# Two stage entries of a fused fp32-accurate kernel: the last chunk of X turned through VectorE and DMAs, and the first two jobs alternating

## Chip, cores and metric

The kernel runs on one core of one Trainium2 chip. The metric is the device time of one execution in microseconds; the median of three runs is given.

## What is computed

One sequence of 256 tokens, model width 2048, all in float32, goes through a retention layer, a pooling layer, an RMS norm, a block with two kinds of attention, a cross-attention to 256 memory tokens, a gated feed-forward layer and a last RMS norm. What matters for the change are the two places where the running sum x is normalised and enters the next projection:

```python
h = h + retention_layer(h, ...)          # ends in  o @ w_out
h = h + pooling_layer(h, ...)            # begins with rms_norm(h) @ w_in ; ends in @ w_out
x = rms_norm(h, final_norm)
# second block
h = rms_norm_2(x, g_mix); proj = h @ w_in    # dq, dk, dv, c_q, c_kv, k_rope
```

## The kernel before, in words

**Products.** X (256 tokens by 2048) stays in SBUF, in two tiles of 128 tokens. Every float32 product is made of three fp32r products: weights are split into `hi` (ScalarE, `split_hi`, L671) and `lo` = raw - hi (VectorE, `split_lo`, L1173), the activation, turned so that its 2048 features lie on partitions, into `xh` and `xl`. A **job** is 512 output columns for both token tiles (two PSUM banks). A **unit** is 512 rows of weight for one job, 1 MB, in two halves; `unit` (L1983) issues 12 matmuls of 512 columns for each half, 24 for a unit: hi with xh (L1998), hi with xl (L1999), lo with xh (L2004). Jobs alternate between two PSUM pairs (`J % 2`), so a third job can start only when the first is drained.

**Look-ahead.** `hi` and `lo` have four places, one for each half: ScalarE may split half H once TensorE has used half H-4 (`half_used`), which is two units of look-ahead. ScalarE and VectorE run their instructions in program order; whatever waits in their stream holds back the splits that stand behind it. Weights are loaded by SyncE into four raw buffers when `lo` of four units earlier is done.

**Entries.** Two stages end in an output projection of 8 units (4 jobs of 2 units) that adds to X, and are followed by a stage whose products need the new X turned: the entry of pooling (`m=0`) and the entry of the input projections of the second block (`m=1`). In this text an entry's units are counted from the first unit of the output projection: units 0 to 7 are the output projection, 8 to 11 are the first job of the next stage, 12 to 15 the second, 16 to 19 the third. X is turned in four chunks of 512 columns; chunk c is final when unit 2c+1 ends. A chunk can be turned in two ways.

- *Across* (chunks 0 to 2): VectorE adds the job to X (`accumulate`, L1229) and transposes it in blocks of 32 by 32 (`blocks`, L1220); GpSimd writes the blocks to DRAM (`turn_across`, L617, 512 KB) and, once they are there, reads them back in four DMAs (L621, 128 KB each) into a free tile; ScalarE makes `xh` (`x_across`, L697) and sums squares of the chunk (`square`, L657); VectorE makes `xl` (`x_crossed`, L1209). ScalarE waits at `x_across` for the reads to land.
- *By TensorE* (chunk 3): eight transposes against the identity into PSUM (`turn_block`, L2022), which stand between the units 9 and 10; then `turn_two` on ScalarE (L681, L682) and VectorE (L1185).

**Order.** `turn_tail` says behind which split each chunk is taken up on ScalarE and VectorE: chunk 0 behind that of unit 6, chunk 1 behind 8, chunk 2 behind 10, chunk 3 behind 11. `first_job_crossed` (L2120) issues units 8 to 11 with chunk 0, 1, 2 and 3 in this order and so waits for one new chunk at each. Behind chunk 3 the sum of squares is closed: VectorE's `invert` (L1232), ScalarE's `root` (L723), and in pooling a wait of ScalarE for it, ahead of the split of unit 12. In the second entry the chain is longer: split of unit 12, root R1, split of 13, VectorE multiplies all of X by R1 and the final norm's gain (L1604, eight instructions), ScalarE squares two chunks, splits unit 14, squares two more, root R2, splits unit 15, and drains the first job.

**Pooling's first group.** The first job (512 columns of u) is drained by ScalarE (L712), turned across by `turn_group`, and copied into `upad` by `pad_group` (L861), where ScalarE waits for its reads.

## Time and profile before

| | |
|---|---|
| three runs, median | 2506.39 us (2505.79 to 2506.41) |
| the profiled execution, its time | 2508.08 us |
| the profiled execution, its span | 2506.3 us |
| TensorE matmul busy | 2493.3 us, 99% of the span, 11088 instructions |
| VectorE busy | 1577.5 us, 63% |
| ScalarE busy | 1214.2 us, 48% |
| GpSimd busy | 185.9 us, 7% |
| queue of SyncE's DMAs | 477.32 MB, 58.9% of 16 engines |
| queue of GpSimd's DMAs | 63.98 MB, 9.3% of 16 engines |
| granted TensorE clock, mean | 0.999 |

Busy shares are means over the whole span. A row of a timeline gives the start in us from the start of the span, the time from the start to the end of the group, engine, line, operation, tiles and how many instructions are merged; in brackets the idle time just ahead of it and what ended it. Matmuls are pipelined, so a matmul's own duration overlaps the next one's.

### The profile page before, as it was taken

Reading aid. Unit: us, or ns where it says so; the run is one execution under the profiler, and the core shown is the slowest. Engines: PE = TensorE matmul, PEld = TensorE weight load, DVE = VectorE, ACT = ScalarE, POOL = GpSimd, SP = SyncE. Lnnn points to the kernel's source line nnn. Section 1 sums busy time; section 2 is a strip of 40 time slices with the busy share of each in tenths; the row PEclk is TensorE's granted clock in tenths of the full one; section 3 lists DMA queues with packets and bytes.
Section 4 is the critical chain, followed back from the end, with each engine's and each line's share of the span. In section 5 each row is a group of like instructions: output and inputs, shape, how many; then the busy total and the mean of one; then the engine's idle time right before and its main releaser. Section 6 shows DMA issues by size and latency. Waiting matters only on the chain.

```text
span 2506.3 us, 29305 instructions
## 1 busy us (share of the span) xinstructions
PE 2493.3 (99%) x11088; PEld 2060.9 (82%) x11088; DVE 1577.5 (63%) x1970; ACT 1214.2 (48%) x1531; POOL 185.9 (7%) x309
## 2 busy tenths in 40 slices
PE   9999999999999999999999999999999999999998
PEld 7888788888888888888888888888888888888887
DVE  7565665665666666675767766776655555555556
ACT  6454444444445453444545556465544444444444
POOL 0010000000010100000001100010100000000000
PEclk9999999999999999999999999999999999999999
DMA  9676666666687877776777754675766666666664
GB/s 330 206 229 212 212 210 204 217 208 199 218 235 227 243 223 230 228 233 210 218 244 243 238 163 152 229 228 192 237 216 210 201 209 218 203 215 204 214 205 146
DMA packets 261740, 542.81 MB, mean 217 GB/s; under 512 B 13440, under 2 KB 19712, under 8 KB 261248
## 3 DMA queue, kind: packets, MB, share of 16 engines
q1 hardware_dynamic: 240992, 477.32, 58.9%
q0 software_dynamic: 20496, 63.98, 9.3%
q8 instruction: 69, 1.13, 0.2%
q14 instruction: 39, 0.32, 0.0%
q10 hardware_dynamic: 144, 0.06, 0.0%
HBM read 507.23 MB, written 34.08 MB: 216 GB/s over the span
## 4 chain that ended last, share of the span: by engine, by line
PE 98%; DVE 1%; DMA 1%; ACT 0%; issue 0%; POOL 0%; ACTq 0%; DVEq 0%
PE job L1998 31%; PE job L1999 31%; PE job L2004 31%; PE group L2022 1%; DMA rqn<-across 0%; PE att L2292 0%; PE att L2043 0%; PE att L2293 0%; PE group L2314 0%; PE att L2188 0%; PE att L2057 0%; PE att L2056 0%; PE att L2053 0%; PE att L2036 0%; DMA across<-rtmp 0%; PE att L2173 0%
## 5 line engine op out<-in xcount | busy, mean ns | idle before, releaser
L1173 DVE TENSOR_TENSOR lo<-raw,hi 128x1024 fp32r<-128x1024 f32 (+1 forms) x880 | 1054.8, 1215 | 665.8 <-ACT hi L671 650.2
L671 ACT ACTIVATE hi<-raw 128x1024 fp32r<-128x1024 f32 (+1 forms) x880 | 921.9, 1055 | 1111.3 <-PE job L2004 1101.9
L1998 PE MATMUL job<-hi,xh 128*128 128x512 f32 (+1 forms) x2272 | 888.0, 391 | 1.9 <-DVE xl L1209 1.6
L1999 PE MATMUL job<-hi,xl 128*128 128x512 f32 (+1 forms) x2272 | 881.5, 388 | 0.0
L2004 PE MATMUL job<-lo,xh 128*128 128x512 f32 (+1 forms) x2272 | 605.1, 388 | 0.0
L1998 PEld LDWEIGHTS job<-hi,xh 128*128 128x128 f32 x2272 | 426.4, 188 | 92.6 <-issue 3.0
L1999 PEld LDWEIGHTS job<-hi,xl 128*128 128x128 f32 x2272 | 426.9, 188 | 88.4 <-issue 2.1
L2004 PEld LDWEIGHTS job<-lo,xh 128*128 128x128 f32 x2272 | 425.6, 188 | 87.5
L1998 PE MATMUL job<-hi,ah 128*128 128x512 f32 x832 | 326.1, 392 | 0.0
L1999 PE MATMUL job<-hi,al 128*128 128x512 f32 x832 | 323.9, 389 | 0.0
L2004 PE MATMUL job<-lo,ah 128*128 128x512 f32 x832 | 222.5, 389 | 0.0
L1998 PEld LDWEIGHTS job<-hi,ah 128*128 128x128 f32 x832 | 156.1, 188 | 32.9 <-issue 0.4
L2004 PEld LDWEIGHTS job<-lo,ah 128*128 128x128 f32 x832 | 156.2, 188 | 32.5
L1999 PEld LDWEIGHTS job<-hi,al 128*128 128x128 f32 x832 | 156.3, 188 | 32.1
L1229 DVE TENSOR_TENSOR X<-job,X 128x512 f32<-128x512 f32 x168 | 108.0, 684 | 77.4 <-PE job L2004 77.3
L1998 PE MATMUL job<-hi,mh 128*128 128x512 f32 (+1 forms) x400 | 155.4, 388 | 0.0
L1999 PE MATMUL job<-hi,ml 128*128 128x512 f32 (+1 forms) x400 | 154.0, 385 | 0.0
L2004 PE MATMUL job<-lo,mh 128*128 128x512 f32 (+1 forms) x400 | 105.3, 385 | 0.0
L1999 PEld LDWEIGHTS job<-hi,ml 128*128 128x128 f32 x400 | 75.2, 188 | 14.1
L1998 PEld LDWEIGHTS job<-hi,mh 128*128 128x128 f32 x400 | 75.1, 188 | 14.2
L2004 PEld LDWEIGHTS job<-lo,mh 128*128 128x128 f32 x400 | 74.8, 188 | 14.4
L617 POOL DMA_DIRECT2D across<-fblk x11 | 7.9, 723 | 590.9 <-DVE fblk L1871 532.0
(330 smaller groups left out, 1215.1 us busy)
## 6 DMA issues: line engine op xcount, KB each, us to landing
raw<-in_ret_w_in SPq DMA_DIRECT2D x95, 1024.0 KB, 5.2
raw<-in_pool_w_in SPq DMA_DIRECT2D x64, 1024.0 KB, 6.2
raw<-in_w_gate SPq DMA_DIRECT2D x44, 1024.0 KB, 5.2
raw<-in_w_up SPq DMA_DIRECT2D x44, 1024.0 KB, 5.1
raw<-in_w_down SPq DMA_DIRECT2D x44, 1024.0 KB, 5.0
raw<-in_ret_w_out SPq DMA_DIRECT2D x32, 1024.0 KB, 5.1
raw<-in_pool_w_out SPq DMA_DIRECT2D x32, 1024.0 KB, 5.3
raw<-in_w_in SPq DMA_DIRECT2D x28, 1024.0 KB, 5.6
```

Source lines behind the costliest of these rows:

```text
L617: pool.dma_start(across[n % 2].rearrange("(t p) q c -> p t (q c)", p=P), blk.rearrange("p t q c -> p t (q c)")).then_inc(t_out, 16)
L671: act.activation(hi[:, (U.at * 2 + h) % HS, :, 0:n], src, ACT.Copy).then_inc(hi_ready, 1)
L1173: dve.tensor_tensor(lo[:, (U.at * 2 + h) % LS, :, 0:n], src, hi[:, (U.at * 2 + h) % HS, :, 0:n].bitcast(F32), ALU.subtract).then_inc(lo_re ...
L1229: ins = dve.tensor_tensor(xs, pair[J % 2][t][:, :], xs, ALU.add)
L1998: pe.matmul(o, oh[:, kt, ts], w, start=first and k == 0, stop=False)
L1999: pe.matmul(o, ol[:, kt, ts], w, start=False, stop=False)
L2004: ins = pe.matmul(pair[J % 2][t][:, 0:n], oh[:, kt, ts], lo[:, H % LS, k, 0:n], start=False, stop=last and k == 1)
L2022: ins = pe.transpose(gbank[G % 2][:, at:at + P], src(t, c), ident[:, :])
```

## The change

Chunk 3 of both entries goes across as well, into tiles that are free by then (`rkn`, and the second half of `pg`). The sixteen transposes on TensorE and their copies go; two `blocks` pairs and two crossings (each one write and four reads on GpSimd's queue) come. The positions at which ScalarE and VectorE take up the chunks stay: behind the splits of units 6, 8, 10 and 11. The first two jobs of each entry alternate unit by unit (`first_jobs`): units 8 and 9 use chunk 0, units 10 and 11 chunk 1, 12 and 13 chunk 2, 14 and 15 chunk 3; SyncE loads the weights in the new order. The first job so ends with unit 14 and the second with unit 15, and drains, the first crossing of pooling's u, `pad_group` and the rotary steps of the second block are moved behind that.

```diff
-        xL = [[landed(rqT[:, :, :]), landed(rkT[:, :, :]), landing(rqn[:, :, :])],
-              [landing(pz[:, 0]), landing(pz[:, 1]), landing(pg[:, 0])],
+        xL = [[landed(rqT[:, :, :]), landed(rkT[:, :, :]), landing(rqn[:, :, :]), landing(rkn[:, :, :])],
+              [landing(pz[:, 0]), landing(pz[:, 1]), landing(pg[:, 0]), landing(pg[:, 1])],
...
-        def turned_behind(c, units, crossing=False):
-
-
-            if crossing:
-                return (2 * units + 1, 3 * units + 1, 4 * units + 1, 4 * units + 2)[c]
-            return (2 * units, 3 * units, 4 * units, 4 * units + 1)[c]
+        def turned_behind(n):
+
+            return (6, 8, 10, 11).index(n) if n in (6, 8, 10, 11) else None
...
                 for c in range(2):
-                    for j in range(2):
-                        for u in range(4):
-                            load(U + (8 * c + 4 * j + u), rows(w_pi, 512 * u, g * POOL_GW + (2 * D * c + NB * j)))
+                    for n in range(8):
+                        j, u = (n % 2, n // 2) if first and c == 0 else (n // 4, n % 4)
+                        load(U + (8 * c + n), rows(w_pi, 512 * u, g * POOL_GW + (2 * D * c + NB * j)))
...
+            for u in range(4):
+                for j in range(2):
+                    load(Pos(WU + 2 * u + j), rows(w_in[0], 512 * u, W_COLS[j]))
             for j, col in enumerate(W_COLS):
                 n = CKV_N if j == 7 else NB
-                for u in range(4):
+                for u in range(4 if j > 1 else 0):
                     load(Pos(WU + 4 * j + u), rows(w_in[0], 512 * u, col, n), n=n)
...
-            def turn_stage(m, chunks=range(3)):
+            def turn_stage(m, chunks=range(4)):
                 for c in chunks:
                     turn_across(NX[m] + c, x_blk[m], xL[m][c])
...
-            turn_stage(2, range(4))
+            turn_stage(2)
             turn_stage(3, range(1, 4))
...
-            def turn_tail(U, G, gain, col, units, ahead, m=None):
-
-
-
-                for n in range(4 * units + 4):
-                    if n >= ahead:
-                        split_hi(U + n)
-                    for c in range(4):
-                        if n - 1 == turned_behind(c, units, m is not None):
-                            if m is not None and c < 3:
-                                x_across(m, c, gain, col)
-                            else:
-                                turn_two(G - (0 if m is None else 6), c, gain, col)
-
+            def turn_tail(U, gain, col, m):
+
+                for n in range(2, 12):
+                    split_hi(U + n)
+                    c = turned_behind(n)
+                    if c is not None:
+                        x_across(m, c, gain, col)
...
-                    if u == 1:
+                    if u == 1 and not first:
                         drain(J, U, lambda t: un[:, 0, t, :], RS)
-                        if not first:
-                            turned_high(NP + 4 * i - 1, pgT[1], ah, 4)
+                        turned_high(NP + 4 * i - 1, pgT[1], ah, 4)
                 U, J = U + 4, J + 1
                 for u in range(4):
                     split_hi(U + u)
+                    if first and u == 0:
+                        drain(J - 1, U - 1, lambda t: un[:, 0, t, :], RS)
                     if u == 1:
                         drain(J, U, lambda t: un[:, 1, t, :], RS)
+                    if u == (2 if first else 1):
                         pad_group(i, 0)
...
-            drain(Pos(WJ), Pos(WU + 4), lambda t: wn[:, 0, t, :], RS)
+            drain(Pos(WJ), Pos(WU + 7), lambda t: wn[:, 0, t, :], RS)
...
-            def turn_tail(U, J, G, Q, gain, col, units, ahead, crossed=0, m=None):
-
-
-                for n in range(4 * units + 4):
-                    if n >= ahead:
-                        split_lo(U + n)
-                    for j in range(4):
-                        end = units * (j + 1) + (crossed if j == 0 else 0)
-                        if n == end:
-                            accumulate(J + j, U + end, j)
-                            if m is not None and j < 3:
-                                wait_drained(dve, J + j)
-                                blocks(NX[m] + j, x_blk[m], X[:, :, NB * j:NB * (j + 1)])
-                    for c in range(4):
-                        if n - 1 == turned_behind(c, units, m is not None):
-                            if m is not None and c < 3:
-                                x_crossed(m, c, gain, col)
-                            else:
-                                skipped = 0 if m is None else 6
-                                turn_two(G - skipped, Q - skipped, c, gain, col)
-
+            def turn_tail(U, J, gain, col, m):
+
+                for n in range(2, 12):
+                    split_lo(U + n)
+                    if n % 2 == 0 and n <= 8:
+                        c = n // 2 - 1
+                        accumulate(J + c, U + n, c)
+                        wait_drained(dve, J + c)
+                        blocks(NX[m] + c, x_blk[m], X[:, :, NB * c:NB * (c + 1)])
+                    c = turned_behind(n)
+                    if c is not None:
+                        x_crossed(m, c, gain, col)
...
                 if not first:
                     turned_low(TP + 2 * i - 1, pgT[1], al, ah, 4)
-                turn_group(i, 0, J)
+                    turn_group(i, 0, J)
                 split_lo(U + 2)
                 split_lo(U + 3)
                 U = U + 4
                 for u in range(4):
                     split_lo(U + u)
+                    if first and u == 0:
+                        turn_group(0, 0, J)
                     if u == 2:
                         turn_group(i, 1, J + 1)
-                    if u >= 2:
+                    if first and u == 3:
+                        window(0, 0, 0)
+                    if u >= 2 and not first:
                         for s in range(2 * (u - 2), min(2 * (u - 2) + 2, i + 1)):
                             window(i, 0, s)
...
-            rope_block(0, 0)
...
-                    if at == (2, 0):
-                        rope_block(0, 1)
+                    if j == 2:
+                        rope_block(u // 2, u % 2)
                     if at == (2, 1):
                         turn_rope_block(0)
-                    if u in (1, 2) and j <= 4:
+                    if at == (3, 0):
+                        turn_rope_block(1)
+                    if u in (1, 2) and 3 <= j <= 4:
                         rope_block(j - 1, u - 1)
-                    if u == 3 and j <= 4:
+                    if u == 3 and 3 <= j <= 4:
                         turn_rope_block(j - 1)
...
-            def out_and_turn(U, J, G, units, oh=ah, ol=al, k0=0, awaited=lambda j, u: None, behind=lambda n: None,
-                             order=None, turned=None, crossing=False):
-
-
-
-                order = order or [(j, u) for j in range(4) for u in range(units)]
-                for n, (j, u) in enumerate(order):
+            def out_jobs(U, J, oh, ol, k0=0, awaited=lambda j, u: None, behind=lambda n: None, order=None, turned=None):
+
+                for n, (j, u) in enumerate(order or [(j, u) for j in range(4) for u in range(2)]):
                     if turned is not None and j == 0:
                         pe.wait_ge(t_low, turned - 1 + u)
-                    unit(U + n, J + j, oh, ol, k0 + 4 * u, start=u == 0, stop=u == units - 1, groups=awaited(j, u))
+                    unit(U + n, J + j, oh, ol, k0 + 4 * u, start=u == 0, stop=u == 1, groups=awaited(j, u))
                     behind(n)
-                    if j >= 2 and u == 0 and not crossing:
-                        wait_drained(pe, J + (j - 2))
-                        turn_x(G, j - 2)
-
-            def first_job(U, J, G, JD):
+
+            def first_jobs(U, J, m):
 
                 for u in range(4):
-                    unit(U + u, J, xh, xl, 4 * u, start=u == 0, stop=u == 3, groups=G + 2 * u)
-                    if u < 2:
-                        wait_drained(pe, JD + (2 + u))
-                        turn_x(G, 2 + u)
-
-            def first_job_crossed(U, J, G, JD, m):
-
-                for u in range(4):
-                    unit(U + u, J, xh, xl, 4 * u, start=u == 0, stop=u == 3, groups=G if u == 3 else Pos(6 * m + 2 * u),
-                         filled=group_done if u == 3 else xt_low)
-                    if u == 1:
-                        wait_drained(pe, JD + 3)
-                        turn_block(G, lambda t: X[:, t, :], NB * 3)
+                    unit(U + 2 * u, J, xh, xl, 4 * u, start=u == 0, stop=u == 3, groups=Pos(X_PARTS[m] + 2 * u), filled=xt_low)
...
-            out_and_turn(Pos(OUT1_U), Pos(OUT1_J), Pos(OUT1_G), 2, mh, ml, turned=TP, crossing=True)
...
                 if first:
-                    first_job_crossed(U, J, G - 2, Pos(OUT1_J), 0)
-                else:
+                    first_jobs(U, J, 0)
+                for j in range(0 if first else 2):
                     for u in range(4):
-                        unit(U + u, J, xh, xl, 4 * u, start=u == 0, stop=u == 3)
-                U, J = U + 4, J + 1
-                for u in range(4):
-                    unit(U + u, J, xh, xl, 4 * u, start=u == 0, stop=u == 3)
-                U, J = U + 4, J + 1
+                        unit(U + (4 * j + u), J + j, xh, xl, 4 * u, start=u == 0, stop=u == 3)
+                U, J = U + 8, J + 2
...
-            first_job_crossed(Pos(WU), Pos(WJ), Pos(OUT2_G), Pos(OUT2_J), 1)
+            out_jobs(Pos(OUT2_U), Pos(OUT2_J), mh, ml, turned=TF)
+
+
+            first_jobs(Pos(WU), Pos(WJ), 1)
...
-            for j in range(1, 8):
+            for j in range(2, 8):
```

The order of instructions shows it at three places.

On ScalarE at the first entry, before, from the split of unit 10 to that of unit 12 (`hi<-raw` is a half of a split, `xh<-rqn` the taking up of crossed chunk 2, `xh<-group` that of chunk 3 out of PSUM):

```order
L671 ACTIVATE hi<-raw 128x1024 [waits half_used]
L697 ACTIVATE xh<-rqn,gain 128x256 [waits t_in]
L697 ACTIVATE xh<-rqn,gain 128x256 x3
L657 ACTIVATE junk,stat<-X 128x512 [waits squares] x2
L671 ACTIVATE hi<-raw 128x1024 [waits half_used,raw_landed3]
L671 ACTIVATE hi<-raw 128x1024 [waits half_used]
L681 ACTIVATE xh<-group,gain 128x256 [waits group_filled]
L682 ACTIVATE xh<-group,gain 128x256
L681 ACTIVATE xh<-group,gain 128x256 [waits group_filled]
L682 ACTIVATE xh<-group,gain 128x256
L657 ACTIVATE junk,stat<-X 128x512 [waits squares] x2
L723 ACT_TABLE_LOAD
```

and now, with the split of unit 12 at the end:

```order
L696 ACTIVATE xh<-rqn,gain 128x256 [waits t_in]
L696 ACTIVATE xh<-rqn,gain 128x256 x3
L656 ACTIVATE junk,stat<-X 128x512 [waits squares] x2
L670 ACTIVATE hi<-raw 128x1024 [waits half_used,raw_landed3]
L670 ACTIVATE hi<-raw 128x1024 [waits half_used]
L696 ACTIVATE xh<-rkn,gain 128x256 [waits t_in]
L696 ACTIVATE xh<-rkn,gain 128x256 x3
L656 ACTIVATE junk,stat<-X 128x512 [waits squares] x2
L722 ACT_TABLE_LOAD
L722 ACTIVATE stat<-stat 128x2 [waits inverse]
L670 ACTIVATE hi<-raw 128x1024 [waits half_used,raw_landed0,rms_ready]
```

In the place of the wait for TensorE's transposes (`group_filled`) stands a wait for chunk 3's reads (`t_in`), behind the split of unit 11 and ahead of that of unit 12.

On VectorE at the same entry, now, behind unit 8 (`X<-job` is the addition of chunk 3):

```order
L1167 TENSOR_TENSOR lo<-raw,hi 128x1024 [waits half_used,hi_ready] x4
L1223 TENSOR_TENSOR X<-job,X 128x512 [waits half_used]
L1223 TENSOR_TENSOR X<-job,X 128x512
L1214 STREAM_TRANSPOSE rtmp<-X 128x4x4x32 [waits t_out,drained1]
L1214 STREAM_TRANSPOSE rtmp<-X 128x4x4x32
L1203 SCALAR_TENSOR_TENSOR xl<-rkT,gain,xh 128x256 [waits xt_high]
```

The two block transposes are new there; before, the step of chunk 1 (`xl<-rkT`) followed the addition at once.

On ScalarE in pooling's third job, now, from the second half of unit 16's split:

```order
L670 ACTIVATE hi<-raw 128x1024 [waits half_used]
L711 ACTIVATE un<-job,stat 128x512 [waits half_used]
L711 ACTIVATE un<-job,stat 128x512
L670 ACTIVATE hi<-raw 128x1024 [waits half_used,raw_landed1]
L670 ACTIVATE hi<-raw 128x1024 [waits half_used]
L711 ACTIVATE un<-job,stat 128x512 [waits half_used]
L711 ACTIVATE un<-job,stat 128x512
L670 ACTIVATE hi<-raw 128x1024 [waits half_used,raw_landed2]
L670 ACTIVATE hi<-raw 128x1024 [waits half_used]
L853 ACTIVATE upad<-un 128x4x256 [waits t_in]
```

The two drains stand one unit apart, and the copy that waits for the first one's crossing is two units behind its drain. Before, it stood four units behind it.

## Rows read from the trace of the kernel before

**Rows 1.** The page: busy time of the engine, granted clock in 40 slices.

```profile
PE 2493.3 (99%) x11088; PEld 2060.9 (82%) x11088; DVE 1577.5 (63%) x1970; ACT 1214.2 (48%) x1531; POOL 185.9 (7%) x309
...
PEclk9999999999999999999999999999999999999999
```

**Rows 2.** TensorE's waits, whole span, the one at an entry: total, times, longest.

```profile
PE job L1998 <- DVE xl L1209: 1.6, 1, 1.6
```

**Rows 3.** Timeline of TensorE at the first entry, units 9 and 10.

```profile
743.40 1.07 PE L2004 MATMUL job<-lo,xh 128*128 128x512 f32 x4
...
746.12 1.08 PE L2004 MATMUL job<-lo,xh 128*128 128x512 f32 x4
747.03 1.04 PE L2022 MATMUL group<-ident,X 128*128 128x128 f32 x8
749.66 0.50 PE L1998 MATMUL job<-hi,xh 128*128 128x512 f32 x1 [1.59 <-DVE xl L1209]
750.00 0.39 PE L1999 MATMUL job<-hi,xl 128*128 128x512 f32 x1
```

**Rows 4.** Timeline of TensorE at the second entry, the same place.

```profile
1359.11 1.03 PE L2022 MATMUL group<-ident,X 128*128 128x128 f32 x8
...
1360.21 0.40 PE L1999 MATMUL job<-hi,xl 128*128 128x512 f32 x1
```

**Rows 5.** Timeline of VectorE, chunks 2 and 3 at the first entry.

```profile
726.79 1.30 DVE L1220 STREAM_TRANSPOSE rtmp<-X 128x512 f32<-128x512 f32 x2
...
736.35 1.29 DVE L1229 TENSOR_TENSOR X<-job,X 128x512 f32<-128x512 f32 x2 [2.15 <-PE job L2004]
```

**Rows 6.** Timeline of GpSimd at the first entry: chunk 2.

```profile
728.39 0.72 POOL L617 DMA_DIRECT2D across<-rtmp  x1 [3.96 <-DVE rtmp L1220]
735.08 2.32 POOL L621 DMA_DIRECT2D rqn<-across  x4 [5.97 <-DMA across<-rtmp]
```

**Rows 7.** Timeline of ScalarE at the first entry, chunks 1, 2 and the root.

```profile
732.91 1.71 ACT L697 ACTIVATE xh<-rkT,gain 128x256 fp32r<-128x256 f32 x4 [0.94 <-DMA rkT<-across]
...
747.79 1.70 ACT L697 ACTIVATE xh<-rqn,gain 128x256 fp32r<-128x256 f32 x4 [4.94 <-DMA rqn<-across]
...
750.77 1.99 ACT L671 ACTIVATE hi<-raw 128x1024 fp32r<-128x1024 f32 x2
...
755.59 1.28 ACT L723 ACT_TABLE_LOAD   x1
...
757.12 2.96 ACT L671 ACTIVATE hi<-raw 128x1024 fp32r<-128x1024 f32 x3
```

**Rows 8.** Timeline of GpSimd at the second entry, chunk 2.

```profile
1340.46 0.72 POOL L617 DMA_DIRECT2D across<-pblk  x1 [2.75 <-DVE pblk L1220]
1347.49 2.32 POOL L621 DMA_DIRECT2D pg<-across  x4 [6.31 <-DMA across<-pblk]
```

**Rows 9.** Timeline of ScalarE at the second entry, chunk 2 and the chain behind.

```profile
1355.32 1.71 ACT L697 ACTIVATE xh<-pg,gain_in 128x256 fp32r<-128x256 f32 x4 [0.39 <-DMA pg<-across]
...
1365.63 1.06 ACT L671 ACTIVATE hi<-raw 128x1024 fp32r<-128x1024 f32 x1 [1.50 <-PE job L2004]
...
1368.57 1.04 ACT L671 ACTIVATE hi<-raw 128x1024 fp32r<-128x1024 f32 x1
...
1376.08 0.64 ACT L657 ACTIVATE junk<-X 128x512 f32<-128x512 f32 x1 [3.94 <-DVE X L1604]
...
1378.97 2.00 ACT L671 ACTIVATE hi<-raw 128x1024 fp32r<-128x1024 f32 x2
```

**Rows 10.** Timeline of VectorE at the second entry, X multiplied by R1.

```profile
1373.31 5.38 DVE L1604 SCALAR_TENSOR_TENSOR X<-X,stat,dqT 128x512 f32<-128x512 f32 x8
```

**Rows 11.** Timelines of ScalarE and GpSimd, the first job of pooling.

```profile
761.87 1.25 ACT L712 ACTIVATE un<-job,stat 128x512 f32<-128x512 f32 x2
...
767.07 0.72 POOL L617 DMA_DIRECT2D across<-pblk  x1 [29.67 <-DVE pblk L1220]
775.35 2.32 POOL L621 DMA_DIRECT2D un<-across  x4 [7.55 <-DMA across<-pblk]
```

More of the change, by code:

```diff
@@ L319, in build @@
         OUT1_U, OUT1_J = RU - 8 + 32 * RET_PAIRS, RJ - 4 + 10 * RET_PAIRS
-        OUT1_G, OUT1_Q = RG, 0
-        PU, PJ, PG, PQ = OUT1_U + 8, OUT1_J + 4, OUT1_G + 2, OUT1_Q + 2
+        PU, PJ, PG, PQ = OUT1_U + 8, OUT1_J + 4, RG, 0
         def pool_at(i):
@@ L378, in build @@
         NX1 = 4 * RET_PAIRS
-        NP = NX1 + 3
+        NP = NX1 + 4
         NX2 = NP + 4 * POOL_GROUPS
-        ND = NX2 + 3
+        ND = NX2 + 4
         NQ = ND + 4
@@ L849, in _ @@
             split_hi(Pos(OUT1_U + 1))
-            turn_tail(Pos(OUT1_U), Pos(OUT1_G), gain1, G_POOL, 2, 2, m=0)
+            turn_tail(Pos(OUT1_U), gain1, G_POOL, 0)
             root(RS, MS, 2)
@@ L915, in _ @@
             split_hi(Pos(OUT2_U + 1))
-            turn_tail(Pos(OUT2_U), Pos(OUT2_G), gain_in, 0, 2, 2, m=1)
+            turn_tail(Pos(OUT2_U), gain_in, 0, 1)
             split_hi(Pos(WU + 4))
@@ L1470, in _ @@
             accumulate(Pos(OUT1_J - 1), Pos(OUT1_U), 3)
-            turn_tail(Pos(OUT1_U), Pos(OUT1_J), Pos(OUT1_G), Pos(OUT1_Q), gain1, G_POOL, 2, 2, m=0)
+            turn_tail(Pos(OUT1_U), Pos(OUT1_J), gain1, G_POOL, 0)
             invert(2)
@@ L1593, in _ @@
             accumulate(Pos(OUT2_J - 1), Pos(OUT2_U), 3)
-            turn_tail(Pos(OUT2_U), Pos(OUT2_J), Pos(OUT2_G), Pos(OUT2_Q), gain_in, 0, 2, 2, m=1)
+            turn_tail(Pos(OUT2_U), Pos(OUT2_J), gain_in, 0, 1)
             split_lo(Pos(WU + 4))
@@ L2112, in first_job @@
-            def first_job(U, J, G, JD):
+            def first_jobs(U, J, m):
                 for u in range(4):
-                    unit(U + u, J, xh, xl, 4 * u, start=u == 0, stop=u == 3, groups=G + 2 * u)
-                    if u < 2:
-                        wait_drained(pe, JD + (2 + u))
-                        turn_x(G, 2 + u)
-            def first_job_crossed(U, J, G, JD, m):
-                for u in range(4):
-                    unit(U + u, J, xh, xl, 4 * u, start=u == 0, stop=u == 3, groups=G if u == 3 else Pos(6 * m + 2 * u),
-                         filled=group_done if u == 3 else xt_low)
-                    if u == 1:
-                        wait_drained(pe, JD + 3)
-                        turn_block(G, lambda t: X[:, t, :], NB * 3)
+                    unit(U + 2 * u, J, xh, xl, 4 * u, start=u == 0, stop=u == 3, groups=Pos(X_PARTS[m] + 2 * u), filled=xt_low)
+                    unit(U + (2 * u + 1), J + 1, xh, xl, 4 * u, start=u == 0, stop=u == 3)
@@ L2129, in _ @@
             pe.wait_ge(ident_in, 16)
-            out_and_turn(Pos(OUT1_U), Pos(OUT1_J), Pos(OUT1_G), 2, mh, ml, turned=TP, crossing=True)
+            out_jobs(Pos(OUT1_U), Pos(OUT1_J), mh, ml, turned=TP)
             def pool_turn(i):
-                U, J, G, _ = pool_at(i)
+                U, J, _, _ = pool_at(i)
                 first = i == 0
                 if first:
-                    first_job_crossed(U, J, G - 2, Pos(OUT1_J), 0)
-                else:
+                    first_jobs(U, J, 0)
+                for j in range(0 if first else 2):
@@ L2163, in _ @@
                 pool_turn(i)
-            out_and_turn(Pos(OUT2_U), Pos(OUT2_J), Pos(OUT2_G), 2, mh, ml, turned=TF, crossing=True)
-            first_job_crossed(Pos(WU), Pos(WJ), Pos(OUT2_G), Pos(OUT2_J), 1)
+            out_jobs(Pos(OUT2_U), Pos(OUT2_J), mh, ml, turned=TF)
+            first_jobs(Pos(WU), Pos(WJ), 1)
             def diff_scores(h):
@@ L2341, in _ @@
                 behind_output(n)
-            out_and_turn(Pos(OUT3_U), Pos(OUT3_J), Pos(OUT3_G), 2, mh, ml,
+            out_jobs(Pos(OUT3_U), Pos(OUT3_J), mh, ml,
                          awaited=lambda j, u: (Pos(LG + 6 * u + 2), Pos(LG + 6 * u + 5)) if j == 0 else None,
-                         behind=lambda n: behind_output(8 + n), order=OUT3_ORDER, crossing=True)
+                         behind=lambda n: behind_output(8 + n), order=OUT3_ORDER)
             def of_memory(u):
@@ L2353, in _ @@
                 unit(Pos(XQU + u), Pos(XJ + 1), xh, xl, 4 * u, start=u == 0, stop=u == 3,
-                     groups=Pos(12 + 2 * u), filled=xt_low)
+                     groups=Pos(X_PARTS[2] + 2 * u), filled=xt_low)
                 if u == 0:
```

8 lines of the change are left out of this document (4 added, 4 removed).

## Prediction

> **What bounds the kernel.** The page's first part is read first: matmuls fill 99% of the span at a granted clock of nine tenths or more in every slice [rows 1]. So only two things can shorten the kernel: matmuls taken away, and gaps of TensorE. The list of TensorE's waits shows that at the entries there is one, 1.6 us [rows 2]. The timelines of the other engines then tell how much room each has there.
>
> Two halves of a unit end 2.72 us apart (743.40 to 746.12), so a unit takes 5.44 us; one matmul follows another after 0.227 us [rows 3]. Unit 10 of the first entry would begin at 747.03 and its second matmul at 747.26; that one comes at 750.00. Transposes and wait together cost **2.74 us** [rows 3]. At the second entry the same count is 1359.11 + 0.23 = 1359.34 against 1360.21: **0.87 us** [rows 4]. That is all there is to win: 3.61 us, 0.14% of the kernel. A measurement of this kernel tells about 0.2%, 5.0 us, from no change.
>
> **What is removed.** Sixteen transposes and the 1.6 us wait: -2.74 and -0.87 us, if nothing takes their place. Unit 10 now needs chunk 1, which ScalarE took up at 732.91, and unit 12 chunk 2, taken up at 747.79 [rows 7]; unit 12 would begin at 747.03 + 10.88 = 757.91. Both are there in time.
>
> **What is added on VectorE and GpSimd.** Two block transposes at each entry, 1.30 us [rows 5], in place of nothing on TensorE's path: the next `lo` comes 1.3 us later, and VectorE had waited 2.15 us for a unit just ahead of the addition [rows 5], so it is not behind. Cost 0. The steps that make `xh` and `xl` of chunk 3 replace equal ones. The new order of loads moves no byte. Cost 0.
>
> **The wait that is added** decides. ScalarE takes up chunk 3 behind the split of unit 11; until its reads have landed, the split of unit 12 stands behind it. Chunk 3 is final only at 747.03 - 10.88 = 736.15, and unit 12 wants its split at 757.91, 21.8 us later. Chunk 2 needed from its end at 725.27 to 747.79: 22.5 us. So the question is when chunk 3 arrives.
>
> *Arrival at the first entry.* The addition starts at 736.35 and takes 1.29, the transposes 1.30: blocks ready at 738.9; the write is issued at 739.2 (chunk 2: transposes 726.79 to 728.09, issue 728.39, 0.3 later) [rows 5, 6]. Chunk 2's reads are still under way then, and they arrive at 747.79. GpSimd's DMAs seem to follow each other: chunk 2's own write was done at 735.08, 2.2 us after chunk 1's reads were taken up at 732.91, and took 6.7 us for it [rows 6, 7]. The write of chunk 3 then is done at 747.8 + 1.6 = 749.4 (1.6 is my choice between 1 and 2.2). Bounds: 739.2 + 6.7 = 745.9 if it waits for nothing, 750.0 with 2.2. The four reads took 12.7 us from first issue to the taking up at the first entry (735.08 to 747.79), and 7.8 at the second (1347.49 to 1355.32) [rows 6, 8, 9]. I take 8.1 here, near the short end, because VectorE and ScalarE are held up by chunk 2 until 750 and so free no raw buffer: few loads compete. Arrival **757.5**.
>
> *What it holds back.* Taking up and squaring lasts 747.79 to 750.77, 2.98 us; from the end of the squares to the split behind the root 755.59 to 757.12, 1.53; half a split 1.06 [rows 7]. The split of unit 12 is ready at 757.5 + 5.6 = 763.1, where TensorE would have begun at 757.91: **a new wait of about 5.2 us**. Before, unit 12 began at 750.00 - 0.23 + 10.88 = 760.65. Difference: **+2.5 us**. With arrivals from 753.7 (nothing waited for, short reads) to 762.7 it is -1.3 to +7.7.
>
> *Second entry.* Chunk 3 is final at 1359.11 - 10.88 = 1348.23, the write is issued 3.05 us later at 1351.3; chunk 2 arrives at 1355.32; write done at 1356.9; reads 8.4 (its neighbour took 7.8) [rows 8, 9]: arrival **1365.3**. Unit 12 has no root ahead of it: its split is ready at 1365.3 + 2.98 + 1.06 = 1369.3, wanted at 1359.11 + 10.88 = 1369.99. No wait. But the chain behind starts later. From the arrival: first half of unit 12's split starts at +3.0, `lo` of both halves until +6.4, R1 and then the split of 13 at +7.1 (before, 2.94 us from the second half of the split of 12 to that of 13), `lo` of 13 done at +10.4, X times R1 starts; 2.77 us later ScalarE squares (1373.31 to 1376.08), 2.89 us on it splits 14 (1376.08 to 1378.97), ready 1.06 later: +17.2, 1382.5 [rows 9, 10]. TensorE now wants it at 1369.99 + 10.88 = 1380.87; before, unit 14 began at 1360.21 - 0.23 + 21.76 = 1381.74. Difference **+0.8**, and 0.2 for the split of 15, which the same chain brings a little late, an estimate: **+1.0 us**. Arrivals of 1363.5 to 1369.6 give -0.9 to +5.3.
>
> *Pooling's first group.* The first job ends with unit 14, so at the start P of unit 15; the second half of 16's split can start then: 1.06, drain 1.25, transposes 1.30, 0.4 of hand-over, write 8.3 at most (767.07 to 775.35), reads 7.8: P + 20.1; copy and half a split of about 1.06 each make 22.2, against 21.76 when unit 19 wants it [rows 11]. Cost **+0.4 us**; with a write of 6.7 it is nothing, with reads of 12.7 it is 5.3. The rotary steps of the second block come one or two units later on VectorE, in front of a first use six units on; cost 0.
>
> **Sum.** +2.5 + 1.0 + 0.4 = **+3.9 us**: 2512.0 for the profiled execution of 2508.08, which lies 1.7 us above the median. Against the median 2506.39 it is **2510.3 us**, +0.16%, within what can be told from no change. The transposes' time is won and more than that is lost behind ScalarE.
>
> A rule on the write's time speaks for the change. The Trainium skill, DMA: Bandwidth & Descriptors, section on the SWDGE path, fits one DMA with 2.0 us plus one for each 436 KB, an estimate of 3.2 us for the 512 KB and 2.3 for each read. By it chunk 3 would arrive before 748 and the sum would be -3.6 us. The rows contradict it under load: 6.7, 7.0 and 8.3 us for the write.
>
> **Rivals.**
>
> 1. *Slow reads: slower.* The place is ScalarE's wait for chunk 3 at both entries; it costs a us for each us past 755.0 and 1364.5. With reads of 10.3 us, the middle of the two seen, to 12.7 at both, +4.7 to +7.1 and +2.7 to +5.2, with pooling's group 1 to 3: **+8 to +15 us**, 2514.8 to 2521. The total passes 5.0 when the reads take about 8.8 us at each. For it: 12.7 us at the first entry [rows 6, 7]. Against: 7.8 at the second, and the loads pause. Chance 0.33.
> 2. *The clock falls in the new wait.* TensorE would stand still for 5 us, longer than any wait of this trace, where the clock stayed at its higher level [rows 1, 2]. A unit at half the clock costs 5.44 us more; one at most, since work resumes at once: +0 to +5.4 over the forecast, say **2513** to 2516. Chance 0.07. The Trainium skill, TensorE: Matmul & The Clock Gate, section on why this matters, has the rule that a gap between matmul bursts brings the clock back to its lower level; no run here shows it yet.
> 3. *The write does not wait for the reads ahead of it.* Then arrival at 753.7 to 756.7 and about 1363.5: -1.3 to +1.7 and -0.9; **2504.2 to 2508**. Nothing shows it apart from the short pause between them. Chance 0.14.
> 4. *All of the 3.61 us is kept* and nothing waits: **2502.8**. Chunk 3 would have to arrive by 752.3; no crossing was that quick. It would still count as no change. Chance 0.03; and faster by over 5 us would need a gain that the profile has no place for, 0.02.
>
> The forecast has what is left, 0.41, for +1 to +5.5 us.
>
> **Numbers.** Slower by over 0.2%: rival 1 nearly whole 0.31, rival 2 0.06, the forecast's upper edge 0.04: 0.41. Faster by over 0.2%: 0.03. Within: 0.56. The range leaves out the lower part of rivals 3 and 4 and the upper third of rival 1: 2503.8 to 2517.0.
>
> **What would show it.** Right: TensorE's matmul of unit 12 at the first entry has a wait of 3 to 7 us whose releaser is `hi`; ScalarE sits idle before `xh<-rkn` until about 757 for `rkn<-across`; GpSimd's write of chunk 3 takes about 10 us; at the second entry a short wait at unit 14, none at unit 10. Slow reads: the idle before `xh<-rkn` ends past 760. Wrong: no wait of TensorE at unit 12, or chunk 3 taken up before 752; or a loss elsewhere than at these two entries, for instance at unit 19 of pooling by several us.

## Result, and the profile after

The changed kernel takes **2517.61 us** (median of six runs, 2516.48 to 2518.31) against 2506.4: ratio 1.0044, interval 1.0034 to 1.0054, so 11.2 us slower. The forecast was 2510.3 with a range up to 2517.0: the sign of its sum was right, its size was a third of what came, and the result lies just above the range. The profiled execution took 2517.76 us with a span of 2515.9, 9.6 more than the 2506.3 of before; it is this difference that the rows below have to account for.

The page after, busy times and clock, beside [rows 1]:

```profile
PE 2495.5 (99%) x11072; PEld 2061.2 (82%) x11072; DVE 1580.2 (63%) x1974; ACT 1214.2 (48%) x1531; POOL 192.0 (8%) x319
...
PEclk9999999999999999999999999999999999999999
```

Sixteen instructions fewer on TensorE, as intended, and in the page nothing looks worse. The timeline of TensorE around unit 12 of both entries (start, time to the end of the group; in brackets the idle time ahead and what ended it) shows it, beside [rows 3, 4]:

```profile
756.83 1.07 PE L1994 MATMUL job<-lo,xh 128*128 128x512 f32 x4
763.75 0.76 PE L1988 MATMUL job<-hi,xh 128*128 128x512 f32 x1 [5.85 <-ACT hi L670]
...
768.54 0.39 PE L1988 MATMUL job<-hi,xh 128*128 128x512 f32 x1
...
1374.19 1.07 PE L1994 MATMUL job<-lo,xh 128*128 128x512 f32 x4
1377.68 0.47 PE L1988 MATMUL job<-hi,xh 128*128 128x512 f32 x1 [2.42 <-ACT hi L670]
...
1381.85 0.63 PE L1988 MATMUL job<-hi,xh 128*128 128x512 f32 x1
...
1384.84 0.39 PE L1988 MATMUL job<-hi,xh 128*128 128x512 f32 x1
...
1390.75 0.47 PE L1988 MATMUL job<-hi,xh 128*128 128x512 f32 x1 [0.31 <-ACT hi L670]
```

Unit 12 could begin four matmuls after 756.83, at 757.74, and begins at 763.75: 6.0 us of wait. Its first half then takes 763.75 to 768.54, 4.79 us in place of 2.72: 2.1 us more, with every operand there. At the second entry the wait is 1377.68 - (1374.19 + 0.91) = 2.6 us, the halves take 4.17 and 2.99 (1.7 more), and unit 14 comes 0.5 after 1384.84 + 5.44. What slows the halves is in the windows of TensorE (window, length, busy us and instructions, granted clock, DMA share, GB/s):

```profile
755.00:760.00 5.00, 2.90 (x13) 1.00 0.79 246
760.00:765.00 5.00, 1.25 (x3) 0.61 0.01 6
765.00:770.00 5.00, 5.00 (x17) 0.70 0.54 147
...
1370.00:1380.00 10.00, 7.58 (x32) 0.95 0.39 116
1380.00:1390.00 10.00, 10.00 (x40) 0.88 0.68 210
...
1379.00:1380.00 1.00, 1.00 (x4) 0.50 0.00 0
```

From 765 TensorE is busy throughout and issues 17 matmuls in 5 us instead of 22: its clock is at the lower of its two levels (1.2 GHz, 0.50 in the last row, which lies wholly inside such a stretch) for part of that window. In this kernel the page's row of clocks, tenths over slices of 63 us, cannot show it.

What TensorE waited for is ScalarE's split, and ScalarE had waited for chunk 3's reads. Timeline of ScalarE, beside [rows 7, 9]:

```profile
744.57 1.71 ACT L696 ACTIVATE xh<-rqn,gain 128x256 fp32r<-128x256 f32 x4 [1.89 <-DMA rqn<-across]
...
757.94 1.70 ACT L696 ACTIVATE xh<-rkn,gain 128x256 fp32r<-128x256 f32 x4 [8.39 <-DMA rkn<-across]
...
762.55 3.90 ACT L670 ACTIVATE hi<-raw 128x1024 fp32r<-128x1024 f32 x4
...
1373.52 1.71 ACT L696 ACTIVATE xh<-pg,gain_in 128x256 fp32r<-128x256 f32 x4 [8.04 <-DMA pg<-across]
1376.49 1.99 ACT L670 ACTIVATE hi<-raw 128x1024 fp32r<-128x1024 f32 x2
...
1386.66 0.63 ACT L656 ACTIVATE junk<-X 128x512 f32<-128x512 f32 x1 [4.13 <-DVE X L1593]
...
1389.56 1.99 ACT L670 ACTIVATE hi<-raw 128x1024 fp32r<-128x1024 f32 x2
```

Four half splits run in one piece at 762.55: the places for them had long been free, and they stood behind the wait. Timeline of GpSimd, chunk 3's write (L616) and reads (L620), beside [rows 6, 8]:

```profile
739.10 0.72 POOL L616 DMA_DIRECT2D across<-rtmp  x1 [2.23 <-DVE rtmp L1214]
745.93 2.32 POOL L620 DMA_DIRECT2D rkn<-across  x4 [6.11 <-DMA across<-rtmp]
...
1356.46 0.72 POOL L616 DMA_DIRECT2D across<-pblk  x1 [4.44 <-DVE pblk L1214]
1362.35 2.32 POOL L620 DMA_DIRECT2D pg<-across  x4 [5.17 <-DMA across<-pblk]
```

The write took 6.8 and 5.9 us, the reads 12.0 (745.93 to 757.94) and 11.2 (1362.35 to 1373.52).

**The account**, profiled span: gain -3.6; waits +6.0, +2.6, +0.5; clock +2.1, +1.7: +9.3 of 9.6 us. The remaining 0.3 is not placed.

These terms are read off in the order of time, and at the second entry they are not independent. From the take-up of chunk 3 at 1373.52 to the first half of unit 14's split, ready at 1389.56 + 1.06 = 1390.62, ScalarE waits for VectorE (the longest time is the 4.13 us at 1386.66), VectorE for ScalarE, and neither for TensorE. Unit 14 begins right behind it, at 1390.75. Had the clock not fallen there, TensorE would have been at unit 14 some 1.7 us earlier and would have waited as much longer. So at this entry the 1.7 us did not lengthen the kernel in this execution: the entry cost what ScalarE's chain cost, 2.6 + 0.5 + 1.7 - 0.87 = 3.9 us. At the first entry, where nothing later waits, the clock's 2.1 us count in full.

### The profile page after: what moved, and what is told of

It is laid out like the page before. It is cut to its first block, busy times and chain, and to the rows that moved or that the text cites. A ratio compares the mean times of both kernels' runs of the same rounds, so it can differ in the third digit from the quotient of the medians.

```text
span 2515.9 us, 29287 instructions
## 1 busy us (share of the span) xinstructions
PE 2495.5 (99%) x11072; PEld 2061.2 (82%) x11072; DVE 1580.2 (63%) x1974; ACT 1214.2 (48%) x1531; POOL 192.0 (8%) x319
## 4 chain that ended last, share of the span: by engine, by line
PE 95%; DMA 2%; DVE 1%; ACT 1%; issue 1%; POOL 0%; ACTq 0%; DVEq 0%
PE job L1988 30%; PE job L1989 30%; PE job L1994 30%; PE group L2012 1%; DMA rkn<-across 0%; DMA pg<-across 0%; DMA fT<-across 0%; PE att L2261 0%; PE att L2033 0%; PE att L2262 0%; PE att L2157 0%; PE group L2283 0%; PE att L2047 0%; PE att L2046 0%; PE att L2043 0%
## 5 line engine op out<-in xcount | busy, mean ns | idle before, releaser
L1994 PEld LDWEIGHTS job<-lo,mh 128*128 128x128 f32 x400 | 74.7, 188 | 14.4
L616 POOL DMA_DIRECT2D across<-fblk x11 | 7.9, 722 | 589.0 <-DVE fblk L1861 530.0
```

Source lines behind the costliest of these rows:

```text
L616: pool.dma_start(across[n % 2].rearrange("(t p) q c -> p t (q c)", p=P), blk.rearrange("p t q c -> p t (q c)")).then_inc(t_out, 16)
L1994: ins = pe.matmul(pair[J % 2][t][:, 0:n], oh[:, kt, ts], lo[:, H % LS, k, 0:n], start=False, stop=last and k == 1)
```

## Experiments

The theory after the result had three parts: (A) nothing but the place of ScalarE's and VectorE's take-up of chunk 3 costs time; (B) after the wait the clock costs some 2 us at each entry on top; (C) the reads are slow because the weight loads of the new order run beside them. Rivals: the crossings themselves cost time wherever they are taken up (two more sets of DMAs, VectorE's blocks); the first half of unit 12 is slow for want of data or because of the splits beside it, not of clock; the reads are slow whatever runs beside them; the alternating order, not the crossing, is what costs. The numbers are in one table. Each run is set against runs of the kernel before taken beside it (median 2506.48 for experiments 1, 2, 4 and 6, 2507.22 for 3, 5 and 7).

| run | median, us | against the kernel before beside it, us | ratio and interval | profiled, us (before 2508.08) |
|---|---|---|---|---|
| take-up late, first entry | 2509.54 | +3.1 | 1.0011 [1.0002, 1.0021] | 2509.92 |
| take-up late, both | 2504.84 | -1.6 | 0.9992 [0.9983, 1.0001] | 2504.35 |
| take-up late, second entry | 2512.09 | +4.9 | 1.0017 [1.0007, 1.0027] | 2512.24 |
| TensorE busy in the wait | 2514.95 | +8.5 | 1.0031 [1.0019, 1.0043] | 2516.22 |
| loads held | 2509.78 | +2.6 | 1.0012 [1.0002, 1.0021] | 2506.60 |
| alternating alone | 2506.21 | -0.3 | 0.9999 [0.9990, 1.0008] | 2506.41 |
| crossing alone (four runs, the others six to eleven) | 2521.21 | +14.0 | 1.0047 [1.0031, 1.0064] | 2520.68 |

**1. Chunk 3 taken up two splits later at the first entry.** ScalarE (and VectorE alike with `split_lo` and `x_crossed`):

```diff
-            return (6, 8, 10, 11).index(n) if n in (6, 8, 10, 11) else None
+            return (6, 8, 10).index(n) if n in (6, 8, 10) else None
             turn_tail(Pos(OUT1_U), gain1, G_POOL, 0)
+            for n in range(12, 14):
+                split_hi(Pos(OUT1_U + n))
+            x_across(0, 3, gain1, G_POOL)
```

The second entry stays as changed. Expected:

> The changed kernel, with chunk 3 taken up at the first entry behind the split of unit 13 in place of 11, on ScalarE and VectorE; the second entry is left as changed. Theory A (ScalarE's wait for chunk 3 holds the split of unit 12, and the standstill of 6.0 us brings the clock down for 2.1 us more): TensorE's wait at unit 12 goes, the clock of 760 to 770 stays at 1.0, and the time falls by 6.0 + 2.1 = 8.1 us, from 2517.6 to about 2509.5. Theory B (the loss is made by the longer traffic of the crossing and the later drains, and ScalarE's wait only shows it): the wait turns up again at unit 13 or 14, where chunk 3 is needed, and the time stays within 2 us of 2517.6.

Timeline of its ScalarE:

```profile
759.23 1.69 ACT L696 ACTIVATE xh<-rkn,gain 128x256 fp32r<-128x256 f32 x4
```

Windows of its TensorE at both entries:

```profile
760.00:765.00 5.00, 5.00 (x24) 1.00 0.96 303
...
1370.00:1380.00 10.00, 10.00 (x38) 0.83 0.60 187
```

Timeline of its TensorE, unit 12 of the second entry:

```profile
1369.69 0.47 PE L1996 MATMUL job<-hi,xh 128*128 128x512 f32 x1 [2.19 <-ACT hi L670]
```

ScalarE finds chunk 3 there at 759.23 without any idle time; the wait at the first entry is gone and so is the fall of the clock there. 8.1 us come back (from +11.2 to +3.1), the 6.0 and 2.1 of the account. The second entry still has its wait, and 38 matmuls in 10 us instead of 44.

**2. Taken up later at both entries.** At the second entry chunk 3 goes behind the split of unit 12 (one split later), and the splits of units 14 and 15 go ahead of the squares and of root R2. To the edit above, at the second entry, on ScalarE (VectorE: `split_lo(WU + 4)` ahead of `x_crossed`):

```diff
-            x_across(1, 3, gain_in, 0)
             split_hi(Pos(WU + 4))
+            x_across(1, 3, gain_in, 0)
             root(R1, MS, 3)
             split_hi(Pos(WU + 5))
+            split_hi(Pos(WU + 6))
...
-                if n == 0:
-                    split_hi(Pos(WU + 6))
-            root(R2, MS, 4)
             split_hi(Pos(WU + 7))
+            root(R2, MS, 4)
```

> As the run before, and at the second entry chunk 3 behind the split of unit 12, the split of 14 ahead of the squares of the renewed X and the split of 15 ahead of root R2. Theory A: the wait of 2.6 us at unit 12 of the second entry and the clock's fall of 1.7 us behind it go, and at units 14 and 15 at most 0.5 us stays: 2517.6 - 8.1 - 4.6 = about 2505 us or a little less, which is before's time less what is left of the transposes' 3.6 us. The count from before gives 2506.4 - 3.6 + 0.5 = 2503.3. Theory B: 2512 or more.

Timeline of its ScalarE:

```profile
1364.16 1.71 ACT L696 ACTIVATE xh<-pg,gain_in 128x256 fp32r<-128x256 f32 x4 [1.16 <-DMA pg<-across]
```

Windows of its TensorE:

```profile
760.00:765.00 5.00, 5.00 (x24) 1.00 0.90 285
...
1370.00:1380.00 10.00, 10.00 (x46) 1.00 0.35 107
```

TensorE has no wait at either entry. The profiled execution is 3.7 us under that of before, the 3.61 us that the prediction called all there is to win. Both crossings and the alternating order are in this kernel, so neither costs anything by itself that these runs can tell: the first rival falls. It beats the changed kernel by 12.8 us; against the kernel before the median is 1.6 us lower, and ten of its eleven runs lie below the fastest of 29 of the kernel before (2505.71), but the interval just reaches 1.0001: a gain of this size is at the edge of what can be told.

**3. The late take-up at the second entry alone**, to split the 12.8 us from the other side (edit: that of 2 without that of 1).

> The changed kernel with the second entry alone reordered as in e2_late_both; the first entry waits as changed. If the two entries' losses are separate, the fall from 2517.6 is that between e1_late_first and e2_late_both, 4.7 us: 2512.9. The trace shows the wait of about 6 us at unit 12 of the first entry and none at the second. If part of the second entry's loss came from the first (a queue that stays behind), it is 2511 or less.

From +11.2 to +4.9, 6.3 us, beside 8.1 for the first entry alone: 14.4 where both at once gave 12.8. The two entries' costs add up within 1.6 us. Timeline of its TensorE at both entries:

```profile
762.08 0.77 PE L1991 MATMUL job<-hi,xh 128*128 128x512 f32 x1 [4.02 <-ACT hi L670]
...
1387.65 1.20 PE L1997 MATMUL job<-lo,xh 128*128 128x512 f32 x4 [0.92 <-DVE lo L1168]
```

The wait at the first entry, which this edit does not touch, was 4.0 us in this execution and not the 6 expected, with reads of 10.0 us (746.26 to 756.25); at the second entry none is left at unit 12, but one of 0.9 us for VectorE's `lo` stands where none was expected. Wait and clock together cost 4.0 + 2.5 us at the first entry here, against 6.0 + 2.1 in the changed kernel's profiled execution: a figure for one entry moves by such amounts from one execution to the next.

**4. TensorE kept busy during the wait.** Ahead of unit 12 of the first entry, 22 matmuls whose result nobody uses, into an idle bank:

```diff
+                    if m == 0 and u == 2:
+                        pe.wait_ge(att_read, 6 * RET_PAIRS)
+                        for n in range(22):
+                            pe.matmul(abank[1][:, :], ah[:, n % 8, 0:P],
+                                      al[:, 2 * (n % 4):2 * (n % 4) + 2, :].rearrange("p k s -> p (k s)"),
+                                      start=n == 0, stop=n == 21)
```

> The changed kernel, with 22 matmuls of 512 columns on operands that lie ready, into an idle bank, put on TensorE ahead of unit 12 of the first entry, where it stands still for 6.0 us. They take 22 x 0.227 = 5.0 us and delay nothing. If the first half of unit 12 takes 4.79 us in place of 2.72 because of the standstill before it, the clock stays at 1.0, the half takes 2.72 and the time falls by 2.1 us, to 2515.5. If the slow half has another cause (the operands' arrival, contention on the way to them), the half stays at 4.8 us and the time stays.

Timeline of its TensorE:

```profile
757.89 5.15 PE L2101 MATMUL att<-al,ah 128*128 128x512 f32 x22
763.14 0.47 PE L1988 MATMUL job<-hi,xh 128*128 128x512 f32 x1
765.98 0.39 PE L1988 MATMUL job<-hi,xh 128*128 128x512 f32 x1
```

Window of its TensorE:

```profile
760.00:765.00 5.00, 4.90 (x22) 1.00 0.01 6
```

Unit 12 waits for the same split, and its first half takes 2.84 us instead of 4.79, with the same splits and loads beside it. So the 2.1 us were the clock, (B), at the first entry; at the second no such run was made, and by the account above its fall was not on top there. The median falls by 2.7 us, the profiled time by 1.5: at the second entry this execution had a wait of 3.33 us, 0.9 longer than that of the changed kernel, and lost 3.0 us to the clock behind it (1376.03 to 1389.91 for two units of 5.44).

**5. Loads held back until chunk 3 is read.** SyncE waits for it ahead of the weights of units 14 and 15 of both entries (at the first entry two tables, 0.5 MB, which the changed kernel loads beside chunk 3's reads, go ahead of that wait):

```diff
...
+                            sp.wait_ge(t_in, 64 * (NX1 + 4))
                         load(U + (8 * c + n), rows(w_pi, 512 * u, g * POOL_GW + (2 * D * c + NB * j)))
...
+                    if u == 3 and j == 0:
+                        sp.wait_ge(t_in, 64 * (NX2 + 4))
                     load(Pos(WU + 2 * u + j), rows(w_in[0], 512 * u, W_COLS[j]))
```

> The changed kernel, with SyncE's loads of the weights of units 14 and 15 held back at both entries until chunk 3 has landed (at the first entry the small tables go ahead of them). Chunk 3 landed 22.0 and 20.2 us after its end, with reads of 12.0 and 11.2 us, where I had counted 8.1 and 8.4. Theory C (the reads are long because weights are loaded beside them): the reads fall to 7 to 8 us, chunk 3 is taken up 3 to 5 us earlier, the wait at unit 12 of the first entry shrinks from 6.0 to 1 to 3 us and the clock's fall with it, the one at the second entry goes: 2508 to 2511. Theory D (the reads' length is their own, small packets and fixed cost): taking up within 1 us of 758 and 1373.5 and a time of 2517, if the late loads hold nothing up.

Timeline of its GpSimd:

```profile
739.38 0.72 POOL L621 DMA_DIRECT2D across<-rtmp  x1 [2.22 <-DVE rtmp L1219]
...
746.24 2.32 POOL L625 DMA_DIRECT2D rkn<-across  x4 [6.13 <-DMA across<-rtmp]
...
1357.80 2.32 POOL L625 DMA_DIRECT2D pg<-across  x4 [6.25 <-DMA across<-pblk]
```

Timeline of its ScalarE:

```profile
754.27 1.71 ACT L701 ACTIVATE xh<-rkn,gain 128x256 fp32r<-128x256 f32 x4 [4.52 <-DMA rkn<-across]
```

Timeline of its TensorE, unit 12 of the first entry:

```profile
760.09 0.47 PE L1993 MATMUL job<-hi,xh 128*128 128x512 f32 x1 [1.91 <-ACT hi L675]
```

Windows of TensorE, the changed kernel first, then this one:

```profile
745.00:757.00 12.00, 12.00 (x54) 1.00 1.02 281
...
745.00:757.00 12.00, 12.00 (x55) 1.00 0.77 194
```

The reads took 8.0 us instead of 12.0, and at the second entry 5.3 (to 1363.14) instead of 11.2: loads beside the reads make them long. The write, which ran before the held loads, stayed at 6.9. The wait at the first entry shrank to 1.9 us and the clock stayed up; at the second entry there is no wait at unit 12. The profiled execution, 1.5 us under before's, is the fastest of ten: the runs lie between 2506.6 and 2513.48, all below the fastest of the changed kernel (2516.48), and the median is above that of before. So 8.0 and 5.3 us are those of a quick execution.

The other half of (C), that it is the *new order* of the loads, is not shown: in experiment 7, which has the order of before, the reads of chunk 3 took 8.9 and 10.6 us, longer than with the loads held, too. What goes with their length in the traces is how much SyncE's queue moved from their first issue to the take-up:

| reads | us | MB on SyncE's queue |
|---|---|---|
| changed, chunk 3, both entries | 12.0, 11.2 | 2.95, 2.75 |
| loads held, chunk 3 | 8.0, 5.3 | 1.19, 0.49 |
| crossing alone, chunk 3 | 8.9, 10.6 | 2.13, 2.33 |
| before, chunk 2 | 12.7, 7.8 | 2.97, 1.54 |

A longer read also sees more traffic pass, so only the second row, in which the loads were held on purpose, shows the direction of cause.

**6. Alternating order alone**: as changed, but chunk 3 turned by TensorE again, behind unit 9.

```diff
...
                     unit(U + (2 * u + 1), J + 1, xh, xl, 4 * u, start=u == 0, stop=u == 3)
+                    if u == 0:
+                        wait_drained(pe, JD + 3)
+                        turn_block(G, lambda t: X[:, t, :], NB * 3)
```

> The alternation of the first two jobs at both entries is kept, with the later drains and loads, and chunk 3 is turned by TensorE as before. Theory A: the wait of 1.6 us at unit 10 of the first entry goes, since chunk 2 is needed two units later, and nothing else moves: 2506.4 - 1.6 = 2504.8, no fall of the clock. Theory B (the alternation itself costs, by the later drain of the first job): above 2508, with a wait of TensorE at the third job.

The profiled execution is 1.7 us faster, and its rows place that between the transposes of the two entries (747.32 to 1357.64, 610.3 us, against 612.1 of [rows 3, 4]): it is the 1.6 us wait of [rows 2]. The median is only 0.3 lower, 2506.2 where 2504.8 was expected. No loss in either: the order is not what costs.

**7. Crossing alone**: the kernel before, with chunk 3 across and no transposes on TensorE, units 8 to 11 still the first job.

```diff
...
-                    unit(U + u, J, xh, xl, 4 * u, start=u == 0, stop=u == 3, groups=G if u == 3 else Pos(6 * m + 2 * u),
-                         filled=group_done if u == 3 else xt_low)
-                    if u == 1:
-                        wait_drained(pe, JD + 3)
-                        turn_block(G, lambda t: X[:, t, :], NB * 3)
+                    unit(U + u, J, xh, xl, 4 * u, start=u == 0, stop=u == 3, groups=Pos(X_PARTS[m] + 2 * u),
+                         filled=xt_low)
```

> The kernel before, with chunk 3 crossed at both entries as in the change, but units 8 to 11 all of the first job: no alternation. Chunk 3 is then needed at unit 11, 16.3 us after its end, while the operands from it are ready some 2 us behind its taking up at 22.0 and 20.2. Waits of 7.7 us at the first entry (units 10 and 11 together) and 5.9 at the second, each with a fall of the clock of about 2 us, less 3.6 us of before: +14, 2520.5 us. ScalarE's splits hold nothing up then, since TensorE is late itself. If alternation were what costs, this kernel would be faster than the changed one, below 2517.6.

Timeline of its TensorE:

```profile
757.22 0.80 PE L1999 MATMUL job<-hi,xh 128*128 128x512 f32 x1 [4.45 <-DVE xl L1210]
...
1375.38 0.79 PE L1999 MATMUL job<-hi,xh 128*128 128x512 f32 x1 [6.10 <-DVE xl L1210]
```

Here TensorE waits for the chunk itself, `xl`, at unit 11, not for a split. The time came as expected (2520.5), but not by its terms: the waits are 4.5 and 6.1 us (7.7 and 5.9 expected), and the clock cost 2.6 and 2.4 behind them (757.22 to 765.28 and 1375.38 to 1383.27 for a unit of 5.44) where 2 each was expected. It loses 2.8 us more than the changed kernel by the medians and by the profiled spans, as it would if alternating hid a part of the crossing; but of its four runs one (2516.65) lies among those of the changed kernel, so the 2.8 us are not sure.

## Why the prediction was wrong

Two steps failed. The time of chunk 3's reads was put at 8.1 and 8.4 us, on the ground that few loads compete with them; they took 12.0 and 11.2 beside 2.95 and 2.75 MB of loads, which at the second entry turned the forecast of +1.0 us into +3.9. And the clock's fall behind a standstill was put at nothing; it cost 2.1 us at the first entry.

**What bounds, and what is to win: right for the profiled execution.** 3.61 us; experiment 2 has 3.7 between profiled executions. The medians of before and of experiment 2 differ by 1.6 only, those of before and of experiment 6 by 0.3 where the profiled times differ by 1.7, and experiment 2's count from before (2503.3) was missed by 1.5. All three would follow if the 1.6 us wait of [rows 2] stood in the profiled execution of before (2508.08) and not in its usual ones (2506.4), with some 2.0 us to win there. Only one trace shows that kernel, so this is a reading and not shown. It touches the forecast: the difference was counted in rows of an execution 1.7 us above the median and added to the median.

**The wait that is added: right in kind.** The matmul of unit 12 waits for `hi`, with ScalarE idle at `xh<-rkn` before it, and experiment 1 takes it away by the place of the take-up alone. At the first entry the take-up came at 757.94 where 757.5 was forecast, by two errors that cancel, which was luck. *The write* was to wait 10.2 us behind chunk 2's reads; it took 6.8. The rule behind that number, done 1.6 us after these reads arrive, fits: they were taken up at 744.57 and the write was done at 745.93. What was wrong is their arrival, taken from before as 747.79. In the nine traces 27 writes were issued while reads were under way for which ScalarE then stood waiting, and each was done 1.3 to 2.8 us after that take-up, none before it. Whether a write waits for the reads or both are slowed by the same traffic, no run separates. *The reads* were to take 8.1, "few loads compete"; they took 12.0. The rest of that step, from the take-up to unit 12, was forecast as 5.6 us and measured as 763.75 - 757.94 = 5.8. So the wait was 6.0 against 5.2.

**The second entry: the larger failure.** +1.0 was forecast, without a wait at unit 12; +3.9 came. From the end of chunk 3 (1353.34) to its take-up passed 20.2 us, not 17.1, the reads' 11.2 against 8.4 nearly all of it. The chain behind was counted right: unit 14 was to begin 17.2 us after the take-up, and 1390.75 - 1373.52 = 17.2. With 3.1 us more ahead of it, 0.8 becomes 3.9. This is rival 1, slow reads, with its place and price at this entry; its sign at the first entry, a take-up past 760, did not come. The nearest row for the reads was chunk 2's 7.8 us at the second entry, and it was no neighbour in traffic: 1.54 MB of loads ran beside it, 2.75 beside chunk 3. The ground given, that VectorE and ScalarE free no raw buffer until 750, did not keep the loads away: the DMA engines are full from 745 to 757 (share 1.02, experiment 5), and nearly idle once TensorE waits (0.01 from 760 to 765).

**The clock: the error of judgement.** The sum had 0 for it and rival 2 a chance of 0.07, although the forecast itself contained a standstill of 5 us, longer than any of the trace before. It came at both entries; at the first it cost 2.1 us, and experiment 4 shows that it is the clock, at the second 1.7 us of TensorE's time that ScalarE's chain would have taken anyway. For this rule the prediction named the Trainium skill, TensorE: Matmul & The Clock Gate, section on why this matters. The traces agree that a gap between matmuls brings the lower level, and show it behind shorter gaps than that section of the Trainium skill gives (2.2 and 2.4 us). The term belonged in the sum, because no row spoke against it.

**The miss, term by term**, from +3.9 to the +9.6 of the profiled spans: second entry +2.9, clock at the first +2.1, wait at the first +0.8, pooling's first group -0.4, not placed +0.3. The medians are 11.2 apart and not 9.6, because the profiled execution of before lies 1.7 us above its median and that of the changed kernel 0.15.

**Pooling's first group**: +0.4 forecast, nothing seen. ScalarE took up `upad` at 800.18 and TensorE did not wait.

```profile
800.18 1.06 ACT L853 ACTIVATE upad<-un 128x1024 f32<-128x1024 f32 x1 [5.90 <-DMA un<-across]
```

**Costs set to 0** (VectorE's blocks, the loads' new order as far as TensorE's operands go, rotary steps): right, by experiment 2. Whether the new order of the loads adds to the reads' time is open; that loads beside them do is shown.

## What to carry to other kernels

On an engine that works in program order and also feeds look-ahead, a wait for a transfer costs nothing as long as what was fed ahead of it lasts; put it behind as many of the feeding steps as the consumer needs meanwhile. Here that was two splits at the first entry, and at the second one split with two more put ahead of the squares; together it was worth 12.8 us. Price a transfer from rows with the same traffic beside it, and give it room: here one took twice as long with the loads beside it (11.2 against 5.3 us), and a row for the same transfer with half the loads beside it (7.8 us) misled the forecast. When two engines are both late for the same step, their delays do not add: find out which of them the step waits for. When a forecast contains a standstill of TensorE longer than any in the trace, the clock's fall belongs into the sum, not among the rivals.

## What had not been expected of the hardware

Standstills of 1.6, 1.9 and 0.9 us left the clock at 1.0; those of 2.2, 2.4, 3.3, 4.0, 4.5, 5.9 and 6.1 us were each followed by a stretch at the lower level. The time lost to the clock did not grow steadily with the standstill: for these seven, in the same order, 1.7, 1.7, 3.0, 2.5, 2.6, 2.1 and 2.4 us, each the time of the next one or two units less 5.44 us each. After the two short ones the clock fell only when work had been resumed for 0.6 to 1.2 us, and stayed down for 3 to 4 us; after the longer ones it was down when work resumed. Four reads of 128 KB each took from 5.3 to 12.7 us; with loads held back beside them they took 5.3 and 8.0, in all others whose landing a waiting ScalarE shows 7.8 or more.
